# Expert weights in 2 MB transfers through four slots, and the last contraction tiles of the down projection in two fp32r parts

## What is computed

```python
logits = x @ w_router + b_router
top_v, top_i = lax.top_k(logits, 2)            # 2 of 8 experts for each token
combine = ...                                  # softmax weights of the two, 0 elsewhere
for e in range(8):
    y = y + combine[..., e:e + 1] * ((silu(x @ w_g[e]) * (x @ w_u[e])) @ w_d[e])
```

## Time and profile before

| | us |
|---|---|
| median of 3 runs (lowest to highest) | 1660.32 (1659.34 to 1661.12) |
| the profiled execution: its time | 1659.13 |
| the profiled execution: its span | 1657.3 |
| busy in the span: PE / DVE / ACT | 1584.7 / 1155.0 / 810.4 |
| mean granted TensorE clock, share of full speed | 0.982 |

### The profile page before, as it was taken

How to read it: one execution, slowest core, us unless ns; L and a number is a source line. 1 busy time by engine, 2 the same in 40 slices (tenths; PEclk the granted TensorE clock), 3 DMA queues, 4 the chain that set the end, 5 groups by cost and what they waited for, 6 DMA issues and landing times.

```text
span 1657.3 us, 20014 instructions
## 1 busy us (share of the span) xinstructions
PE 1584.7 (96%) x7315; PEld 1265.9 (76%) x7315; DVE 1155.0 (70%) x1312; ACT 810.4 (49%) x1093; POOL 178.0 (11%) x115
## 2 busy tenths in 40 slices
PE   8999999999999999999999999789999999999990
PEld 7877777888888888888777788467777777777770
DVE  6888747584444423379887584698888888888886
ACT  5344442253223222163444422667777777777771
POOL 0410005151000000005000060200000000000006
PEclk9999999999999999999999999899999999999995
DMA  5232232325454232222222324399999999999964
GB/s 209 77 101 65 77 113 88 101 68 203 153 193 150 94 123 100 89 73 86 84 77 77 113 90 180 142 392 392 383 360 384 381 376 370 370 374 370 383 235 165
DMA packets 134380, 325.69 MB, mean 197 GB/s; under 512 B 7984, under 2 KB 19632, under 8 KB 133808
## 3 DMA queue, kind: packets, MB, share of 16 engines
q1 hardware_dynamic: 125440, 291.32, 49.8%
q0 software_dynamic: 5440, 20.97, 3.3%
q10 hardware_dynamic: 3440, 12.58, 1.9%
HBM read 300.20 MB, written 24.64 MB: 196 GB/s over the span
## 4 chain that ended last, share of the span: by engine, by line
PE 94%; DVE 3%; ACT 1%; DMA 1%; issue 1%; POOL 0%; SPq 0%; ACTq 0%; DVEq 0%
PE bank L1312 15%; PE bank L1313 15%; PE bank L1314 15%; PE bank L1593 9%; PE bank L1595 9%; PE bank L1594 9%; PE bank L1352 4%; PE bank L1351 4%; PE bank L1350 4%; PE bank L1601 3%; PE bank L1572 1%; PE bank L1424 1%; PE bank L1437 1%; DVE X L1182 1%; PE bank L1409 1%; PE bank L1305 1%
## 5 line engine op out<-in xcount | busy, mean ns | idle before, releaser
L821 DVE TENSOR_TENSOR wlo<-raw,whi 128x1024 fp32r<-128x1024 f32 x170 | 239.0, 1408 | 207.5 <-ACT whi L522 207.2
L1312 PE MATMUL bank<-xth,whi 128*128 128x512 f32 (+1 forms) x976 | 381.5, 391 | 1.8 <-DVE wlo L821 1.8
L1313 PE MATMUL bank<-xtl,whi 128*128 128x512 f32 (+1 forms) x976 | 370.8, 380 | 0.0
L1314 PE MATMUL bank<-xth,wlo 128*128 128x512 f32 (+1 forms) x976 | 370.5, 380 | 0.0
L1045 DVE TENSOR_TENSOR ewlo<-eraw,ewhi 128x2048 fp32r<-128x2048 f32 x135 | 309.0, 2290 | 66.8 <-ACT ewhi L717 66.7
L717 ACT ACTIVATE ewhi<-eraw 128x2048 fp32r<-128x2048 f32 x135 | 258.0, 1911 | 43.0 <-PE bank L1595 43.0
L522 ACT ACTIVATE whi<-raw 128x1024 fp32r<-128x1024 f32 x170 | 178.6, 1051 | 137.0 <-PE bank L1352 123.9
L1312 PEld LDWEIGHTS bank<-xth,whi 128*128 128x128 f32 x976 | 184.2, 189 | 50.7 <-issue 8.5
L1313 PEld LDWEIGHTS bank<-xtl,whi 128*128 128x128 f32 x976 | 184.2, 189 | 36.4 <-issue 3.8
L1593 PE MATMUL bank<-ewhi,xgh 128*128 128x512 f32 (+1 forms) x528 | 205.9, 390 | 6.0 <-DVE xgl L1112 4.8
L1314 PEld LDWEIGHTS bank<-xth,wlo 128*128 128x128 f32 x976 | 184.1, 189 | 35.3
(11 more groups left out here) (235 smaller groups left out, 2230.0 us busy)
## 6 DMA issues: line engine op xcount, KB each, us to landing
eraw<-expert_gu SPq DMA_DIRECT2D x102, 1024.0 KB, 8.2
raw<-dense_w SPq DMA_DIRECT2D x170, 512.0 KB, 3.4
eraw<-expert_dn SPq DMA_DIRECT2D x33, 1024.0 KB, 8.3
erawx<-expert_gu SPq DMA_DIRECT2D x22, 1024.0 KB, 8.3
eplain<-expert_dn SPq DMA_DIRECT2D x22, 768.0 KB, 9.9
erawx<-expert_dn SPq DMA_DIRECT2D x11, 1024.0 KB, 9.3
item_rows<-zero POOLq DMA_DIRECT2D x8, 1024.0 KB, 4.8
rows<-item_rows ACTq DMA_DIRECT2D x11, 512.0 KB, 7.2
```

Source lines behind the costliest of these rows:

```text
L821: V.tensor_tensor(wlo[:, g % SPL, :], raw[:, g % RAW, :], whi[:, g % SPL, :], ALU.subtract).then_inc(lo_done, 1)
L1312: mm(out, wh, xh, start=first, stop=False)
L1313: mm(out, wh, xl, start=False, stop=False)
L1314: return mm(out, wl, xh, start=False, stop=last)
```

## The change

- Gate and up weights of a block land in one transfer of 2 MB with runs of 4 KB (both halves of the contraction at once; the last block 1 MB), and contraction tiles 0 to 7 of each half of the down projection in one of 2 MB with runs of 4 KB. These eight *slabs* of an item go through a ring of four 2 MB slots (three in `eraw`, one in `erawx`); before, it was eight slots of 1 MB. The pieces that ACT, DVE and PE work on stay as they are.
- Pieces 13 and 16 are split as the others. Their weights (768 KB each, the loads "a" and "b") land one after the other in one buffer, `eland`, which lies over constants no longer needed; their parts have a buffer of their own, `eshi`/`eslo`. ACT and DVE do an `e_split` and `e_low` of 1536 columns more for each, DVE also `htl` of the hidden blocks 4 and 5, and PE does nine fp32r matmuls for each in place of three float32 products.
- SP's order in an item is slabs 2, 3, 4, 5, 6, a, 7, b, and then slabs 0 and 1 of the next item. Load b waits until `e_low` of piece 13 is done.
- ACT's order at the end of an item becomes: `e_split` of piece 13, of 14, of 15, `xg_high`, `e_split` of 16, `y_out(0)`, `e_split` of 0, 1 and 2 of the next item, `y_out(1)`. DVE's becomes `e_low` of 13, `htl` of block 4, `e_low` of 14, `htl` of block 5, `e_low` of 15, `xg_low`, `e_low` of 16, and of 0, 1 and 2 of the next item.

```diff
-ERING, EMAIN, ESPL = 8, 6, 3
+SHORT = [13, 16]
+RING = [p for p in range(NPC) if p not in SHORT]
+ERING, EMAIN, ESPL = 4, 3, 3
...
+SLABS = [("gu", b, 4 if b < 5 else 2) for b in range(6)] + [("dn", h, 4) for h in range(2)]
+NSL = len(SLABS)
+LOAD = [0, 1, 2, 3, 4, 5, 6, "a", 7, "b"]
+AHEAD = 2
...
+SLAB_END = [max(p for p in RING if slab_of(p) == i) for i in range(NSL)]
...
-        eraw = at("eraw", [P, EMAIN, EW], F32)
+        eraw = at("eraw", [P, EMAIN, 2 * EW], F32)
...
-        eplain = at("eplain", [P, 2, EW], F32, o)
-        erawx = at("erawx", [P, ERING - EMAIN, EW], F32, o + 2 * EW * 4)
+        eshi = at("eshi", [P, 1536], F32R, o)
+        eslo = at("eslo", [P, 1536], F32R, o + EW * 4)
+        erawx = at("erawx", [P, ERING - EMAIN, 2 * EW], F32, o + 2 * EW * 4)
...
+            def expert_load(e, i):
+
+                if i in ("a", "b"):
+                    h = "ab".index(i)
+                    what, b, n, k0, kn = "dn", h, 4, KD, FET - KD
+                    dst = by_column(eland, SHORT[h])
+                    arrived = in_short
+                else:
+                    what, b, n = SLABS[i]
+                    k0, kn, dst, arrived = 0, KD, slab(i), in_e[i % ERING]
...
+            def slot_free(i, j):
+
+                if i == "a":
+                    if not isinstance(j, int):
+                        sp.wait_ge(e_lo, (j - 1) * NPC + (SHORT[1] + 1))
+                elif i == "b":
+                    sp.wait_ge(e_lo, j * NPC + (SHORT[0] + 1))
+                elif i >= ERING:
+                    sp.wait_ge(e_lo, j * NPC + (SLAB_END[i - ERING] + 1))
+                elif isinstance(j, int) and j == 0:
+                    if i >= EMAIN:
+                        sp.wait_ge(sel_mm, 2)
                 else:
...
+                    sp.wait_ge(e_lo, (j - 1) * NPC + (SLAB_END[i - ERING] + 1))
...
             with sp.Fori(1, turns) as j:
 
                 e = sp.value_load(tab[0:1, bass.ds(j, 1)], min_val=0, max_val=NE - 1)
-                for p in range(ESPL, NPC):
-                    slot_free(p, j)
-                    expert_piece(e, p)
+                for i in LOAD[AHEAD:]:
+                    slot_free(i, j)
+                    expert_load(e, i)
                 e = sp.value_load(tab[0:1, bass.ds(j + 1, 1)], min_val=0, max_val=NE - 1)
-                for p in range(ESPL):
-                    slot_free(p, j + 1)
-                    expert_piece(e, p)
+                for i in LOAD[:AHEAD]:
+                    slot_free(i, j + 1)
+                    expert_load(e, i)
...
+            def e_split(p, j):
+
+                if p in SHORT:
+                    act.wait_ge(in_short, j * 32 + 16 * (SHORT.index(p) + 1))
+                    if p == SHORT[1]:
+                        act.wait_ge(e_used, j * NPC + (SHORT[0] + 1))
+                else:
+                    act.wait_ge(in_e[slab_of(p) % ERING], landed(slab_of(p), j))
...
-                    e_split(p + ESPL, j)
+                    e_split(p + 3, j)
                 hidden_high(4, j)
                 e_split(14, j)
                 hidden_high(5, j)
+                e_split(15, j)
+                xg_high(j + 1)
+                e_split(16, j)
+                y_out(0, j)
                 e_split(0, j + 1)
-                xg_high(j + 1)
-                y_out(0, j)
                 e_split(1, j + 1)
                 e_split(2, j + 1)
                 y_out(1, j)
...
+                hidden_low(4, j)
                 e_low(14, j)
+                hidden_low(5, j)
...
+                e_low(15, j)
+                xg_low(j + 1)
+                e_low(16, j)
                 e_low(0, j + 1)
-                xg_low(j + 1)
                 e_low(1, j + 1)
                 e_low(2, j + 1)
...
-                    else:
-                        i = RAWP.index(p)
-                        pe.wait_ge(in_plain[i], j * 16 + 16)
-                        for kk in range(kn):
-                            k = k0 + kk
-                            ins = mm(out, ht32[:, k - F_SPLIT, :], cols(eplain[:, i], kk), start=(k == 0),
-                                     stop=(k == last - 1))
+                    pe.wait_ge(e_lo, j * NPC + (p + 1))
...
-                pe.wait_ge(ht_hi, j * N_BLK + 6)
+                pe.wait_ge(ht_lo, j * N_BLK + 6)
                 piece(13)
```

More of the change, by code:

```diff
@@ L76, with slab_of @@
 NPC = len(PIECES)
[L77 to L80, removed]
-ERING, EMAIN, ESPL = 8, 6, 3
+SHORT = [13, 16]
+RING = [p for p in range(NPC) if p not in SHORT]
+ERING, EMAIN, ESPL = 4, 3, 3
 EW = 2048
 N_BLK = 6
-LOADS = [len([o for o in range(NSP) if o % ERING == s]) for s in range(ERING)]
+SLABS = [("gu", b, 4 if b < 5 else 2) for b in range(6)] + [("dn", h, 4) for h in range(2)]
+NSL = len(SLABS)
+LOAD = [0, 1, 2, 3, 4, 5, 6, "a", 7, "b"]
+AHEAD = 2
+def slab_of(p):
+    what, b, k0, kn = PIECES[p]
+    return b if what == "gu" else 6 + b
+SLAB_END = [max(p for p in RING if slab_of(p) == i) for i in range(NSL)]
 C_ID, C_BLK, C_MEAN, C_ONE, C_TRI = 0, 128, 256, 384, 512
-C_COS, C_SIN, C_INV = 640, 896, 1152
-C_I8, C_I16 = 1664, 1672
-C_END = 1688
+C_I8, C_I16 = 640, 648
+C_COS, C_SIN, C_INV = 672, 928, 1184
+C_END = 1696
 V_QG, V_KG, V_BG, V_PS, V_BDW, V_CG, V_CB, V_DW = 0, 1, 2, 26, 28, 30, 32, 34
@@ L338, in build_trunk @@
         in_e = [sem(f"in_e{i}") for i in range(ERING)]
-        in_plain = [sem(f"in_plain{i}") for i in range(2)]
+        in_short = sem("in_short")
         e_hi, e_lo, e_used = sem("e_hi"), sem("e_lo"), sem("e_used")
@@ L360, in quarters, with landed, slab, piece_of_slab @@
             return ap.rearrange("p (c n) -> p c n", c=4)
[L362 to L369, removed]
+        def landed(i, j):
+            return j * (16 * NSL // ERING) + 16 * (i // ERING + 1)
+        def slab(i):
+            s, n = i % ERING, SLABS[i][2]
+            t = eraw[:, s] if s < EMAIN else erawx[:, s - EMAIN]
+            return t[:, 0:n * D].rearrange("p (c n) -> p c n", c=n)
+        def piece_of_slab(p):
+            k0, kn = PIECES[p][2:]
+            if p in SHORT:
+                return by_column(eland, p)
+            return slab(slab_of(p))[:, :, k0 * P:(k0 + kn) * P]
+        def parts(p):
+            if p in SHORT:
+                return by_column(eshi, p), by_column(eslo, p)
+            o = RING.index(p) % ESPL
+            return by_column(ewhi[:, o], p), by_column(ewlo[:, o], p)
+        def by_column(t, p):
+            n, kn = SLABS[slab_of(p)][2], PIECES[p][3]
+            return t[:, 0:n * kn * P].rearrange("p (c n) -> p c n", c=n)
         def blk(b):
@@ L475, in slot_free @@
                         sp.wait_ge(sel_mm, 2)
                 else:
[L477 to L483, removed]
+                    sp.wait_ge(e_lo, (j - 1) * NPC + (SLAB_END[i - ERING] + 1))
+            for i in LOAD:
+                slot_free(i, 0)
+                expert_load(0, i)
+                if i == EMAIN - 1:
@@ L706, in _ @@
                 nc.scalar.activation(xrh[:, tt, :], X[:, tt, :], ACT.Copy).then_inc(xr_hi, 1)
[L708 to L717, removed]
+            def e_split(p, j):
+                if p in SHORT:
+                    act.wait_ge(in_short, j * 32 + 16 * (SHORT.index(p) + 1))
[3 more added lines that the diff above has]
+                    act.wait_ge(in_e[slab_of(p) % ERING], landed(slab_of(p), j))
+                    o = RING.index(p)
+                    if o >= ESPL:
+                        act.wait_ge(e_used, j * NPC + (RING[o - ESPL] + 1))
+                    elif not isinstance(j, int):
+                        act.wait_ge(e_used, (j - 1) * NPC + (RING[o - ESPL] + 1))
+                nc.scalar.activation(parts(p)[0], piece_of_slab(p), ACT.Copy).then_inc(e_hi, 1)
             e_split(0, 0)
@@ L1581, in piece @@
                     last = KD if what == "gu" else FET
[L1583 to L1602 removed]
+                    pe.wait_ge(e_lo, j * NPC + (p + 1))
+                    ah, al = (xgh, xgl) if what == "gu" else (hth, htl)
+                    hi, lo = parts(p)
+                    for kk in range(kn):
+                        k, cols = k0 + kk, slice(kk * P, (kk + 1) * P)
+                        mm(out, ah[:, k, :], hi[:, :, cols], start=(k == 0), stop=False)
+                        mm(out, ah[:, k, :], lo[:, :, cols], start=False, stop=False)
+                        ins = mm(out, al[:, k, :], hi[:, :, cols], start=False, stop=(k == last - 1))
                     ins.then_inc(e_used, 1)
```

77 lines of the change are left out of this document (22 added, 55 removed).

## The result

The changed kernel takes 1722.49 us (median of 4 runs, 1720.01 to 1726.04) against 1660.62 us before (1659.34 to 1661.12): a ratio of 1.0379, with a 95% interval of 1.0366 to 1.0392. It is 62 us slower, where 9 were forecast; the time lies above the whole range. The profiled execution has a span of 1718.5 us, 61.2 more than that of before.

A forecast was written before the change was run, and what follows sets the result against it. PE was taken to bound the kernel, with transfers close behind. Costs of 1.5 us at the second item's start, 9 periods of 0.5 and 2.8 at the end sum to 9 us, giving 1669.3 us on the median; range 1658 to 1686.

The forecast's parts named there:

- `htl` before piece 13: Late in each item PE waits for `htl` of block 5, 0.4 us, hidden within the 1.5 us wait for slab 0.
- rival B: At the item's start slab 0 lands in time, PE sets the pace: period 48.5 us, 1649 to 1658 us, chance 0.1.
- Step 1: From PE's start on an item to the end of `e_low` of piece 13 on DVE: 35.94 us.
- Step 2: From DVE's end of `e_low` of piece 13 to SP's issue of load b: 0.18 us.
- step 4: From slab 0's landing through ACT's split and DVE's low part of piece 0 to PE's start: 4.33 us.
- step 3: From load b's issue to slab 0's landing: latency 2.3 us plus 6.87 us for 2.88 MB at 420 GB/s.
- rival D: PE's longer wait at the item's start lowers its clock: 1 to 2 us more a period, 1678 to 1690 us, chance 0.12.
- the slabs behind slab 0 are no later than it: In the next item, slabs land 5.0 us apart and PE uses one in 5.8 us, so they add no wait.
- DVE's 1.5: At the second item's start, `e_low` of piece 0 ends late on DVE, at 1126.6 against 1125.07: costs 1.5 us.
- The tail: In the last item the final store waits for `y_out(1)`, behind a split that needs slab 1: costs 2.8 us.
- A: Rival at load b and slab 0: the link is quick, no change, 1659 to 1666 us, chance 0.2.
- C: Rival on slab transfers: 4 KB runs bring nothing, 386 GB/s stay, PE waits at piece 8, 1674 to 1685 us, chance 0.13.

The follow-up runs named there:

- experiment 1: The changed kernel with load b issued behind slabs 0 and 1 of the next item: 1661.53 us, ratio 1.0013 to the kernel before.
- experiment 3: The kernel before with only pieces 13 and 16 split, 1 MB pieces kept, piece 16's load behind the next item's first three: 1655.08 us, ratio 0.9973.
- experiment 8: experiment 3 with piece 16's load put back ahead of the next item's first pieces in SP's queue: 1685.98 us, ratio 1.0167.
- experiment 9: The changed kernel with SP reading the next item's expert ahead of the wait at load b: 1693.58 us, ratio 1.0206.
- experiment 4: The changed kernel with three unused float32 products on constants behind piece 16 of every item, keeping PE busy: 1712.44 us, ratio 1.0318.
- experiment 10: The changed kernel without load b: SP waits at its place, piece 16 uses piece 13's weights: 1680.87 us, ratio 1.0129.
- experiment 6: experiment 1 with SP, in the first item, holding slab 4 until GpSimd's scattered rows have landed: 1657.04 us, ratio 0.9985.

## Why the prediction was wrong

**What held.** PE's busy time in an item falls from 49.10 to 48.14 us in experiment 1, 0.96 of the 1.06 forecast, and 0.25 us of waiting for `htl` before piece 13 stays (forecast 0.4): period 48.4, rival B's 48.5. The splits of 1536 columns take 1.47 and 1.76 us (1.48 and 1.76), DVE's busy time rises by 3.7 to 3.9 us an item (4.25), ACT's by 2.4 to 2.7 (3). Step 1, 35.94 us, is 35.90 us in experiments 1 and 3. Step 2 is 0.17 us (0.18), and step 4 is 4.29 us (4.33). `e_split`(16) comes right behind `xg_high` without a wait. The mechanism, a wait for slab 0 behind load b, is shown by experiments 1 and 8.

**What failed: step 3.** I had 9.17 us; it took 11.37 us in the item shown, and ACT began piece 0 11.5 to 12.1 us after `e_low`(13) in the nine items, against 9.35. The latency and the rate have a small part in it: with the two loads issued one right behind the other it is 9.73, 0.6 us over. I had taken b and slab 0 as one transfer of 2.88 MB. But SP reads the next item's expert between them, which is a statement of the diff that I quoted and priced at nothing. That costs 1.65 us (1.9 on average over the items). In the kernel before the same read stands ahead of the next item's loads too, but with transfers queued in front of it, so that it cost nothing there.

**What failed behind it.** The wait was 3.1 to 3.8 us, not 1.5, and with that rival D came in too: the clock fell to 0.50 in eight of the nine items. I had counted D as an alternative to the forecast (0.12), though by the earlier trace rows it was the forecast's next step as soon as the wait grew by some tenths. It took more than those tenths: in experiment 9 waits of up to 1.8 us left the clock at 1.00. D's price, 1 to 2 us a period, is met in the five items whose clock was low longest: from PE's start to the next `e_low`(13) they take 38.3 to 38.6 us, against 37.05 in the one item at full clock. Net it is 0.9 us a period on average (experiment 4). And "the slabs behind slab 0 are no later than it" was wrong: I had compared the spacing of the slabs with PE's use of them, where ACT needs slab 1 for piece 2 with four steps queued behind it. From PE's start to the next `e_low`(13) are 37.03 us in experiments 9 and 10, at full clock, instead of 35.94.

**The sum again.** A period was 54.2 us on average, 4.6 above the forecast of 49.6. The gap behind b gives 1.9 (ACT's start on piece 0, changed kernel against experiment 9), the rest of steps 3 and 4 0.5 (14.2 against 13.68), slab 1 1.1, the clock 0.9 to 1.1. The ten periods are 51.1 us over those of before, where the forecast had 6.0 for them (nine of 0.5, and DVE's 1.5 at the end of the first item): 45 of the 52 us that it lacked. DVE's 1.5 us are there, only earlier than forecast. In experiment 3, where no load is late, PE waits for DVE at pieces 13 and 15 of the first item, and the period with these waits is 50.3 us instead of 48.4:

```profile
1114.41 0.49 PE L1611 MATMUL bank<-eshi,hth 128*128 128x512 f32 x1 [1.05 <-DVE htl L1159]
...
1120.07 0.50 PE L1611 MATMUL bank<-ewhi,hth 128*128 128x512 f32 x1 [0.60 <-DVE ewlo L1064]
```

The first item gives 4.7 more, for which the forecast had nothing: the scatter (experiment 6). The tail gives 2.6 more, 5.4 against 2.8, and that is step 3 once more: in the last item slab 1 lands 16.8 us after `e_low`(13), where the forecast had 14.4.

**The other rivals.** A and B needed a faster step 3 and fall with it; B's period does come about once b stands elsewhere. C is wrong: from 1396 on the slabs land at 408 to 422 GB/s against 386 before, and PE has no wait at pieces 4 to 8. The rate just buys nothing (experiments 1 and 3 have the same period). The Trainium skill, DMA: Bandwidth & Descriptors, "Why small descriptors are slow", gives each packet a fixed overhead, by which 4 KB runs would move 395 GB/s, an estimate; the windows show some 5% more, and they decide. The Trainium skill, on the same page in "Anatomy of one DMA", fits a transfer from GpSimd's queue as 2.0 us plus bytes at 436 GB/s, an estimate of 6.8 us for slab 0 alone and 8.6 with b. The runs, from SyncE's queue, give 7.9 and 9.73, and 11.37 where the two issues lie 1.28 us apart; they decide.

## What to carry to other kernels

A load that waits on a shared issuing queue makes every load behind it wait; put the late one last (61 us here for one statement), and place it by what stands behind it, not by its own slot. Where a queue must run dry, count each thing that the issuing engine does between the first loads after it: 0.65 us of scalar work cost 1.65 us of landing and, through PE's wait and its clock, 2.5 us a period. And a rival whose condition lies a few tenths beyond the forecast isn't a rival but its next step: price the two together.

## What the runs showed of the hardware

With slab 0 issued 1.28 us behind b on otherwise idle queues, the engines moved 287 to 343 GB/s for some 6 us, though b was still in flight when slab 0 was issued (b lands 4.3 us after its issue); issued 0.63 us behind b, slab 0 went at 410 to 422. Packet by packet the loss lies in a few: a packet of 4 KB takes 159 ns (median) in both kernels, but up to slab 0's landing 23 to 47 of them an item took over 300 ns behind the longer gap, and 0 to 11 behind the shorter one. With slab 0 alone on idle queues (experiment 10) it is 12 to 34. So behind the longer gap slab 0 starts as on idle queues, and behind the shorter one it doesn't. Why a gap of this size has such an effect isn't settled: the windows show the DMA engines at a share of 0.87 to 0.97 in it, not idle, and no run here varied the gap further. After waits of 3.1 to 3.8 us PE's granted clock fell to the level of 1.2 GHz in eight of nine items, but in one it stayed at 1.00 after 3.3 us (the second line of the item windows above), and waits up to 1.8 us in experiment 9 left it at 1.00; in the first item of before it had fallen after 1.86 us, where a wait of 1.84 us at the same place in the changed kernel's first item left it at 1.00.
